# Neighbourhood-attention heads in one bank each, three units in flight, and the two context blocks of a pair as one unit

## The reference, cut to what matters

```
# neighbourhood heads: 8, in 4 pairs (p = 0..3)
s_win = q . k (window of 8x16 around the query) * scale + bias
s_ctx = q . k_ctx (all 256 context keys) * scale
out   = softmax([s_win, s_ctx]) @ [v_win, v_ctx]
# grouped heads: 8 queries on 2 key heads, in 4 pairs (p = 4..7)
out   = softmax(q . [k_ctx, k] * scale) @ [v_ctx, v]
# in layer 0 alone, the context tokens are queries too, for all 8 pairs
out_c = softmax(q_ctx . k_ctx * scale) @ v_ctx
```

## Time and profile before

| what | value |
|---|---|
| median of 3 runs | 3114.48 us (3113.07 to 3117.52) |
| the profiled execution, its own time | 3104.24 us |
| its span | 3102.4 us |
| PE busy | 2965.5 us, 96% of the span |
| DVE, ACT, POOL busy | 1054.7, 720.8, 221.8 us |
| mean granted PE clock | 0.985 |
| layer 0 attention, first transpose to last value | 1861.33 to 2048.98 us, in four near and four far pairs |
| layer 1 attention | 2668.84 to 2811.27 us |

### The profile page before, as it was taken

How to read it: one execution, slowest core, us unless ns; L and a number is a source line. 1 busy time by engine, 2 the same in 40 slices (tenths; PEclk the granted TensorE clock), 3 DMA queues, 4 the chain that set the end, 5 groups by cost and what they waited for, 6 DMA issues and landing times.

```text
span 3102.4 us, 41544 instructions
## 1 busy us (share of the span) xinstructions
PE 2965.5 (96%) x16894; PEld 1709.1 (55%) x16894; DVE 1054.7 (34%) x2057; ACT 720.8 (23%) x1429; POOL 221.8 (7%) x280
## 2 busy tenths in 40 slices
PE   5999999999999999999998999999999999999998
PEld 2777766777444444444444566665555544774443
DVE  3555554554312134454411236531010312552011
ACT  3334433332200002211002225520000022452000
POOL 0222211112000000000000101000000001100000
PEclk8999999999999999999999999999999999999999
DMA  5000000001433333444321210001111112101222
GB/s 195 22 29 22 29 29 29 23 28 59 150 102 121 133 115 108 155 153 151 106 84 56 76 44 22 1 28 48 48 54 42 53 54 78 42 2 54 68 79 69
DMA packets 59848, 214.07 MB, mean 69 GB/s; under 512 B 6402, under 2 KB 8578, under 8 KB 59443
## 3 DMA queue, kind: packets, MB, share of 16 engines
q1 hardware_dynamic: 42512, 153.11, 15.6%
q0 software_dynamic: 13344, 50.59, 4.8%
q10 hardware_dynamic: 3842, 8.19, 0.7%
HBM read 208.20 MB, written 2.10 MB: 68 GB/s over the span
## 4 chain that ended last, share of the span: by engine, by line
PE 90%; DVE 5%; ACT 2%; issue 2%; DMA 1%; POOL 0%; DVEq 0%; ACTq 0%; SPq 0%
PE psum L348 87%; PE psum L712 2%; DVE arena L1318 1%; DMA arena<-in_ctxT 1%; DVE arena L1593 0%; DVE arena L1301 0%; DVE arena L1298 0%; DVE arena L1306 0%; DMA arena<-in_stream 0%; POOL arena L1728 0%; ACT arena L935 0%; DVE arena L1579 0%; ACT arena L883 0%; ACT arena L1099 0%; PE psum L540 0%
## 5 line engine op out<-in xcount | busy, mean ns | idle before, releaser
L348 PE MATMUL psum<-arena 64*64 64x64 f32 (+6 forms) x16094 | 2870.7, 362 | 125.0 <-ACT arena L883 18.9
L348 PEld LDWEIGHTS psum<-arena 128*128 128x128 f32 (+4 forms) x16094 | 1623.0, 162 | 1352.6 <-issue 1165.5
L1673 DVE SCALAR_TENSOR_TENSOR arena<-arena,psum 128x512 f32<-128x512 f32 x32 | 21.2, 684 | 381.6 <-PE psum L348 381.6
L1428 DVE SCALAR_TENSOR_TENSOR arena<-arena 128x1024 f32<-128x1024 f32 x128 | 149.2, 1221 | 4.5 <-DMA arena<-in_mods 4.3
L1099 ACT ACTIVATE arena<-psum,arena 128x512 f32<-128x512 f32 (+2 forms) x160 | 115.3, 726 | 57.9 <-DVE arena L1585 21.3
L1152 ACT ACTIVATE arena<-psum 128x512 f32<-128x512 f32 x32 | 19.1, 597 | 382.4 <-PE psum L348 382.4
L712 PE MATMUL psum<-arena 128*128 128x128 f32 x704 | 96.5, 281 | 3.3 <-ACT arena L1099 3.1
L1547 DVE COPY arena<-psum 128x512 f32<-128x512 f32 x26 | 18.0, 692 | 238.3 <-PE psum L348 238.3
L712 PEld LDWEIGHTS psum<-arena 128*128 128x128 f32 x704 | 76.5, 141 | 30.7 <-issue 24.4
L1748 POOL DMA_DIRECT2D arena<-in_bias x16 | 8.7, 550 | 1149.4 <-DVE arena L1557 877.7
L1742 POOL DMA_DIRECT2D arena<-in_mods x76 | 40.1, 528 | 682.8 <-DVE arena L1428 682.8
(11 more groups left out here) (206 smaller groups left out, 1368.1 us busy)
## 6 DMA issues: line engine op xcount, KB each, us to landing
arena<-in_stream SPq DMA_DIRECT2D x288, 512.0 KB, 3.6
arena<-in_mods POOLq DMA_DIRECT2D x80, 512.0 KB, 3.6
arena<-in_bias POOLq DMA_DIRECT2D x16, 384.0 KB, 3.9
arena<-in_xT ACTq DMA_DIRECT2D x1, 2048.0 KB, 17.5
out<-arena SPq DMA_DIRECT2D x1, 2048.0 KB, 7.2
arena<-in_conds ACTq DMA_DIRECT2D x1, 1536.0 KB
arena<-arena POOLq DMA_DIRECT2D x4, 384.0 KB, 4.3
arena<-in_ctxT ACTq DMA_DIRECT2D x1, 1024.0 KB, 19.8
```

Of the source, the lines that this page charges most:

```text
L348: return pe.matmul(out, lhsT, rhs, start=start, stop=stop, skip_group_check=True)
L1428: m = stt(mjunk[:, b % 2, :] if x < len(conds) - 1 else slot, slot, 0.5, cb[:, c, :], ALU.mult, ALU.mult, accum_out=dst(x))
```

## The change

- Near units get two banks each, one for each head: first the head's 256 windowed keys and then its 256 context keys. Three near units are in flight on banks 0 to 5, and `scores(u)` waits for unit u - 3, not u - 2. The wait on `at_s1c` goes, and the parts are issued as head 0, head 1, head 0, head 1. Far units stay as they were.
- The two context blocks of a pair become one unit with the same layout: 2 blocks x 256 keys in each head's bank. Layer 0 has 40 units in place of 48. The statistics tensor `st` grows to four columns for each unit of a parity. One DVE reduction gives four maxima; ACT issues four exponentials; PE has 8 transposes and the values of both blocks.
- For near and context units ACT copies head 0's bank (512 columns) to `PT` and DVE copies head 1's. Before, ACT copied two pieces of 256 columns and DVE the middle bank, and context units had only the DVE copy.
- GpSimd's wait before loading the next bias table is renumbered to the same unit as before.

The diff, cut to its core:

```diff
-            ctx_blocks = [(1, b) for b in range(CC)] if l == 0 else []
-            return [(p, q, b) for p in range(2 * PAIRS)
-                    for q, b in [(0, b) for b in (NEAR_ORDER if p < PAIRS else range(XC))] + ctx_blocks]
+            blocks = [(0, b) for b in range(XC)], [(0, b) for b in NEAR_ORDER]
+            return [(p, q, b) for p in range(2 * PAIRS) for q, b in blocks[p < PAIRS] + ([(1, 0)] if l == 0 else [])]
...
-        def score_banks(u):
-            return flat(psum[:, 3 * (u % 2):3 * (u % 2) + 3, :])
+        def score_banks(l, u):
+            near = PAIRS * (XC + 1 - l)
+            at = 2 * ((u - near) % 3) if u < near else 3 * ((u - near) % 2)
+            return flat(psum[:, at:at + 3 if u >= near else at + 2, :])
...
-                    if u >= 2:
-                        pe.wait_ge(s("at_ptx"), x_before(l, u - 1))
-                        pe.wait_ge(s("at_ptc"), g + u - 1)
+                    free = u - 2 if p < PAIRS else u - 1
+                    if free > 0:
+                        pe.wait_ge(s("at_ptx"), tx_before(l, free))
+                        pe.wait_ge(s("at_ptc"), g + free)
...
-                    part(0, score_at(0, 0, near), lo, lo + n)
-                    part(1, SEQ + CTX, SEQ, TOK).then_inc(s("at_s1c"), 1)
-                    part(1, 2 * SEQ, lo, lo + n).then_inc(s("at_sc"), 1)
-                    pe.wait_ge(s("at_s1c"), x_before(l, u) // 2 + 1)
-                    part(0, SEQ, SEQ, TOK).then_inc(s("at_sc"), 1)
+                    if q:
+                        for b2 in range(CC):
+                            for a in range(2):
+                                m = part(a, SEQ + b2 * P, SEQ * a + CTX * b2, SEQ, TOK)
+                                if b2:
+                                    m.then_inc(s("at_sc"), 1)
+                    elif p < PAIRS:
+                        for a in range(2):
+                            part(a, b * P, SEQ * a, NEAR_AT[b], NEAR_AT[b] + NEAR)
+                        for a in range(2):
+                            part(a, b * P, SEQ * a + NEAR, SEQ, TOK).then_inc(s("at_sc"), 1)
+                    else:
+                        part(0, b * P, 0, 0, SEQ)
+                        part(1, b * P, SEQ + CTX, SEQ, TOK).then_inc(s("at_s1c"), 1)
+                        part(1, b * P, 2 * SEQ, 0, SEQ).then_inc(s("at_sc"), 1)
+                        pe.wait_ge(s("at_s1c"), far_before(l, u) + 1)
+                        part(0, b * P, SEQ, SEQ, TOK).then_inc(s("at_sc"), 1)
...
+                    for a in range(2):
+                        pe.wait_ge(s("at_P"), 2 * (g + u) + a + 1)
+                        for c in range(XC):
+                            m = turn(chunk_at(a, c) if far(us[u]) else SEQ * a + c * P)
+                        m.then_inc(s("at_tx" if far(us[u]) or not a else "at_tc"), 1)
...
                 def evict(u):
-                    for a in range(2):
-                        act.wait_ge(s("at_tx"), x_before(l, u) + a + 1)
+                    for a in range(1 + far(us[u])):
+                        act.wait_ge(s("at_tx"), tx_before(l, u) + a + 1)
...
+                        for b2 in range(CC if q else 1):
+                            o = stat(u, a, b2 if q else None)
...
+                            m = f(Pr[:, u % 2, at:at + w], score_banks(l, u)[:, at:at + w], ACT.Exp, scale=-1.0,
+                                  bias=st[:, 0, o:o + 1], accum_out=st[:, 1, o:o + 1])
+                        m.then_inc(s("at_P"), 1)
...
-                        dve.tensor_reduce(st[:, 0, o:o + 2], x[:, SEQ:UNIT].rearrange("p (a c) -> p a c", a=2)[:, :, 0:CTX],
+                        dve.tensor_reduce(st[:, 0, o:o + 4], x[:, 0:2 * SEQ].rearrange("p (n c) -> p n c", n=4),
```

More of the change, by code:

```diff
@@ L217, in build @@
         table = sp2.take(4, 3 * NEAR)
[L218 removed]
+        st = sp2.take(4, 8)
         MG2_AT = sp2.at
@@ L706, in transposes, with values @@
+                def values(u):
                     p, q, b = us[u]
                     near = biased(p, q)
[L708 to L714, removed]
-                        for a in range(2):
[L716 to L728, removed]
                     pe.wait_ge(s("at_ptc"), g + u + 1)
-                    if not q:
-                        pe.wait_ge(s("at_ptx"), x_before(l, u) + 2)
+                    pe.wait_ge(s("at_ptx"), tx_before(l, u + 1))
@@ L753, in values, with weight @@
[L753 to L757, removed]
+                    def weight(a, c):
+                        cols = slice(p * P + HD * a, p * P + HD * a + HD)
+                        if not near or c >= XC:
+                            return VAt[:, c, cols] if p < PAIRS else VBt[:, c, half(a)]
+                        j = NEAR_AT[b] // P + c
+                        return VAs[:, j, cols] if b in (1, 2) else VAt[:, j, cols]
@@ new lines, in prob_at @@
+                    def prob_at(a, c, b2):
+                        if q:
+                            return SEQ * a + CTX * b2 + (c - XC) * P
+                        if near:
+                            return SEQ * a + (c if c < XC else c - XC + NEAR // P) * P
+                        return chunk_at(a, c)
+                    chunks = [*([] if q else range(NEAR // P) if near else range(XC)), XC, XC + 1]
+                    for b2 in range(CC if q else 1):
+                        for c in chunks:
+                            for a in range(2):
+                                at = prob_at(a, c, b2)
+                                m = mm(psum[half(a), 6, (b + b2) * P:(b + b2 + 1) * P], weight(a, c),
+                                       PT[:, u % 2, at:at + P], c == chunks[0], c == CH - 1)
+                                if c == CH - 1 and (not q or b2):
+                                    m.then_inc(s("at_pv"), 1)
@@ L759, in attention @@
+                    pe.wait_ge(s("at_ri"), g + u + 1)
+                    for b2 in range(CC if q else 1):
+                        for a in range(2):
+                            o = stat(u, a, b2 if q else None)
+                            m = mm(psum[half(a), 7, (b + b2) * P:(b + b2 + 1) * P],
+                                   st[:, 2, o:o + 1].to_broadcast([P, HD]), ident)
+                            if not q or b2:
+                                m.then_inc(s("at_rs"), 1)
                 for u in range(len(us) + 2):
```

90 lines of the change are left out of this document (40 added, 50 removed).

## The result

The changed kernel took 3076.92 us in the median of four runs (3071.24 to 3078.33), the kernel before 3114.24 us (3113.07 to 3117.52): a ratio of 0.9875, interval 0.9858 to 0.9892, or 37 us less. In two later comparisons the ratio was 0.9895 (0.9878 to 0.9911: 3077.03 us against 3111.70) and 0.9895 (0.9879 to 0.9912: 3079.89 against 3112.40), 33 to 35 us less. The forecast was 26 us less, 3088 us, and 3080 us at the least. The direction was right, the forecast gain was too small, and the range missed the time.

What follows compares the result with a forecast made beforehand. PE was taken as the bound, held up by order and banks. Gains of 12.0 + 5.7 + 6.8 + 1.5 = 26.0 us off the 3114.48 us median gave 3088 us; forecast range 3083 to 3094, wider range 3080 to 3099.

Steps and rivals of the forecast that it cites:

- What bounds the kernel: PE holds 90% of the chain; in attention it idles 20.5 us, stopped by order and banks, chiefly waits for DVE's copy.
- The scores' order: Near units' score group: four parts, two abreast twice, take 1.26 us for 1.42, a gain of 0.16 us.
- Rival 2: PE packs better: four score parts take 0.95 us, 40 units give 12 us more, about 3076 us; chance 0.07.
- The third slot: Near units' scores wait for a copy one unit older; waits of 0.18 us and those around near pairs' context units vanish.
- The merged unit: Layer 0's merged context unit takes 3.75 us of PE for two at 4.06 before waits, values 1.47, maxima and exponentials hidden.
- The far pairs' 0.2 to 0.3 us of shortage: In layer 0's far pairs, context values leave PE short by this once a pair, behind DVE's late copy: 23.9 us spacing.
- The start: At each attention stage's start, the third slot removes about 0.75 us of the third unit's wait for an eviction: 1.5 us.
- The sum: Attention's gains in near pairs of both layers, far pairs of layer 0 and the starts add to 26.0 us.
- its own bound of 0.95 us: Lower bound for a near unit's four score parts, if today's eight passes fill six equal slots of 0.24 us.
- Slower rivals: In attention, DVE's delays to maxima eat the gain or more: slower has chance 0.05, no change 0.03.
- rival 4: No change: PE idles again wherever released, transposes waiting for exponentials just as long; rival 3 with half its delay; chance 0.03.
- rival 3: Slower: DVE becomes the bound through the write to `ATT`; two delays above 2.3 us in each of 12 pairs; chance 0.05.

Runs made afterwards that it cites:

- the version that goes further: Against the changed kernel, far units' scores cut in parts of 256 keys, issued with equal parts of both heads abreast: 3072.70 us, ratio to before 0.9869.

## Why the prediction was right and wrong

**What bounds the kernel: right.** PE's waits on the copy and PE's own work were the place. The wait went from 11.8 us to 0.3.

**The scores' order: this step failed.** "Twice that is 1.26 us against 1.42: a gain of 0.16 us" took 0.63 us, the time of a group with two parts, as the price of two parts. Of it 0.20 us is the group's own, paid once, and 0.43 the parts'. Four parts take 0.20 + 2 x 0.43 = 1.06 us; the profile has 1.07. The miss is 0.19 us in each of 40 units, 7.6 us, and stands in every spacing: 4 x 0.19 of the 0.74 us by which near pairs of layer 1 came out shorter, 5 x 0.19 of the 0.94 in layer 0. Rival 2 (0.95 us for four parts, 0.07 of chance) was nearest in size, but it lacked the reason, and that its 3076 us is the measured time is luck: at 1.07 us its 12 us become 7.6. The trace of before could have told: of the two pairs of products at 1897.79 the second starts 0.32 us after the first, but within a near unit's group products also start 0.22 us apart (1891.34, 1891.56, 1891.77). Between a group of 20 loads and one of 12 I did divide by the difference (0.055 us a load) and for the scores I did not.

The same error set aside the Trainium skill's rule of up to twice the speed (TensorEngine Tiling (Array Packing), Theoretical Speedup). I held 0.63 us for a pair of parts against the 0.40 that the rule would give. A further pair costs 0.42 to 0.44 us, so by these runs the rule was nearly right for each pair, and the 0.20 us once a group is what stood between. The run with the wait put back has one product of head 1 alone, and the next starts 0.22 us after it (2664.94, 2665.16); two abreast also take 0.22. Within a group, then, the second head was free: twice the speed. The same page of the Trainium skill says (Tiling Modes, Key Properties) that changing the tiling mode drains TensorE, and gives no number; the 0.20 us would fit, but no run here tells a drain from another cause.

**Which part of the change gave this: half right.** I gave the group's gain to "two abreast is just what the new order does". The order is not the price (1.07 us when undone), nor, to 0.02 us, the shared bank as such; the wait for a product's end is: put back alone it makes 1.40 us of the old 1.42. The bank for each head is what lets the wait go.

**The third slot: right as to the wait.** Forecast 0.18 us a unit (5.8 us) and the waits by context units of near pairs; merging alone took most of the latter away (18.90 us for 20.87). Without the slot the stages are 10.2 us longer. That is 0.18 us again in most units, but 0.57 behind a pair's write (the row at 2677.76), where I had worked out that maxima come late and had not followed it to the copy. And 0.9 us of it is the clock at layer 0's start, which costs 2.5 us with two slots (9.37 us against 6.82 in layer 1) and 1.6 with three.

**The merged unit: right.** Values 1.47 us, hidden maxima and exponentials, as worked out. Merging alone, on the kernel before, made the stage 13.8 us shorter: 8.5 us (4 x 2.12) are the far pairs and the rest near pairs. Both stages together took 332.6 us before, 318.7 with merging alone, 311.5 with the two-bank layout and its copies, without the wait inside the scores, as well, and 301.3 with the third slot: 13.9, 7.2 and 10.2 us, together 31.3. In this order merging is the largest part, but the shares hang on the order: taken singly out of the changed kernel, merging is worth 9.0 us, the missing wait 9.1 and the third slot 10.2. The far pairs' 0.2 to 0.3 us of shortage did not appear: 23.50 is the plain sum. (It appears once the far scores are shorter: 0.38 us a pair in the version that goes further.)

**The start: right in layer 1, and in layer 0 the clock was not seen.** Periods alone would give 4 x 3.94 + 4 x 2.12 + 4 x 2.17 = 32.9 us. The stages gave 31.3, so the ends cost 1.6 us where I had added 1.5. Layer 1's first pair write came 18.0 us after the first maxima, for 21.1 before; layer 0's came at 1882.86 - 1863.26 = 19.6, for 21.0. What holds layer 0 is the granted clock. From the first transposes of a stage to those of the third unit, PE has the same work in both layers. These are layer 0 and layer 1 of the kernel before, then of the changed one:

```profile
1861.33:1871.52 10.19, 9.09 (x53) 6.88 (x53) 4.22 (x14) 4.77 (x14) 0.00 (x0) 0.67 0.00 0
2668.84:2676.53 7.69, 6.44 (x52) 4.78 (x52) 4.02 (x14) 4.72 (x14) 0.00 (x0) 1.00 0.01 2
```

```profile
1865.40:1872.69 7.29, 7.28 (x53) 5.29 (x53) 4.22 (x14) 4.49 (x12) 0.00 (x0) 0.77 0.00 0
2649.86:2655.53 5.67, 5.66 (x53) 4.15 (x53) 4.01 (x14) 4.60 (x12) 0.00 (x0) 1.00 0.02 4
```

Layer 0 takes 2.5 us longer than layer 1 before and 1.6 us after, partly at the clock's lower level of 1.2 GHz. So 0.9 us of the 31.3 is clock. The mean clock of 0.96 in the first stretch of the earlier trace rows came from this, and so did the 1.81 us for eight score loads in the earlier trace rows, which are 1.09 at the upper level; the prediction made nothing of either. Why the clock falls here and seldom in layer 1 is not shown: in the changed kernel PE had idled 1.96 us before the fall in layer 0, and 2.02 us at the same place in layer 1, without one.

**The sum.** 26.0 + 7.6 for the scores + 1.0 for the far pairs that did not wait = 34.6, less 3.1 at the ends = 31.5, for 31.3 in the profiles. The first comparison of medians, 37 us, has 31.3 outside its interval (34 to 44 us), the two later ones have it inside. With 1859 to 1873 us for the code ahead of attention, I take the excess for scatter; that is argued, not shown. The range, drawn from 0.63 us and no gain as its two ends, was too narrow on the fast side, for its own bound of 0.95 us led to 3076.

**Slower rivals: rightly set aside.** DVE's busy share did not bind (99.0 of 166.7 us in layer 0), and the exponentials came in time. One slip: rival 4 takes no change for rival 3 with half its delay, but the 2.3 us of rival 3 are what would eat the 26 us, and that is no change already. Where the rows name ACT as what ended the time before the transposes, it is the same 0.33 us between loads as where nothing is named.

## What to carry to other kernels

Before a group of instructions is scaled, take its price apart with two groups of different length: what is left at length nought is paid once. A wait of one product on another inside an engine's own stream costs the end of that product, even where the order looks free; arrange the pieces so that the awaited one ended a piece ago. A copy that frees banks and stands behind other work on its engine is best met by one more slot, even if the units have to be packed tighter for it.

## What the runs showed of the hardware

- Score products of two heads on different halves of the array's rows ran abreast even when issued head after head: 1.07 us for eight products of 256 columns in either order.
- A group of such products had a part of 0.20 us that is there once, whatever its length, up to the first load of the transposes behind it: 0.63, 1.07 and 1.49 us for 4, 8 and 12 products.
- A product of one head alone took 0.22 us to the next start, and two of different heads abreast took 0.22 us too.
- At the start of layer 0's attention the granted clock fell to its lower level for some microseconds in every profile but one: 10.19 us for work that took 7.69 at the upper level, 7.29 for 5.67. In the changed kernel PE had idled 1.96 us before it. The one exception is the kernel with six score parts, where it had idled 1.10 us and the clock stayed at 1.00.
- The same code took 1859 to 1873 us ahead of attention from run to run. Between 850 and 1250 us PE was busy 390.63 us each time, and the mean granted clock was between 0.98 and 0.94, a mixture of its levels of 2.4 and 1.2 GHz.
